# One core, two transformer-like blocks: second down-projection token-major, smaller opening pieces, heads of a pair in turn, a clamp moved to GpSimd

## The chip, the cores and the metric

The kernel runs on one core of one Trainium2 chip. The metric is the device time of one execution in microseconds; the median of three runs of the kernel before is 856.59 us (856.45 to 857.29). Engines are named as the profile names them: PE (TensorE), PEld (its weight loads), DVE (VectorE), ACT (ScalarE), POOL (GpSimd), SP (SyncE, which issues most transfers).

## The reference, cut to what matters

256 tokens of width 1024, all in float32, pass two blocks one after the other. The parts that the change touches:

```python
# first block: the input projection of the gated recurrence
h = rms_norm(x, norm_mix_pre)
z = h @ w_in                     # split into q, f_fwd, f_bwd, i, g, u, v, ga, gb
f = lb + (1 - lb) * sigmoid(zf)  # a gate per direction
logf = log(maximum(f, tiny))     # the clamp
k = (1 - lb) * sigmoid(-zf)
# second block: two attentions of 8 heads each (head width 64; queries and keys 64 or 96 wide)
out_a = dilated_attention(qa, ka, va, rel_bias)
out_b = causal_block_attention(qb, kb, vb)
h = h + concat(out_a, out_b) @ w_o
# second block: the last feed-forward part
hn = rms_norm_2(h, norm_ffn_g)
hid = square(relu(hn @ w_ff1))   # 256 x 4096
return h + hid @ w_ff2           # 256 x 1024
```

## The kernel before, in words

Weights come as 133 units of 128 x 2048 float32 (1 MB each), in the order in which they are used. SP issues their transfers into `raw`, a ring of four slots; unit u waits until unit u-4 is used. Each unit is split into two float32r parts: ACT copies it to `whi` (`split_hi`, L451), DVE subtracts to get `wlo` (`split_lo`, L906). The activations are split in the same way into `xh` and `xl`. PE then makes three products for each block: hi by hi, hi by lo, lo by hi. `ahead(u)` splits the unit three places ahead.

Most products are channel-major: a 128 x 128 block of the weights is loaded and 256 tokens stream past (`mm3`, L1641 to L1643). Some are token-major: 128 tokens of the activations are loaded and 512 weight columns stream past (`token_major`, L1707 to L1713, and `token_down`, L1903 to L1905). In the wide form (`wide_tiles`, L2009 and L2010) hi and lo activations stream together, 512 columns, followed by 256 for `wlo`.

**Opening.** SP issues half of x (512 KB), two halves of unit 0, the other half of x, two halves of unit 1, then whole units. ACT makes `xh` (L476) and `whi` (L502), DVE `xl` (L955) and `wlo` (L987), PE starts with 26 idle products on a tile of ones (L1763) and then runs `first_products`, 48 token-major products for units 0 and 1 (L1752 to L1758). Units 2 and 3 (`zu`) follow channel-major, block by block with all three products together, so they need `wlo` of the unit at their first block. The norm's statistics and its broadcast (`norm_stats`, `norm_bc`) stand inside unit 2 and behind it. Behind unit 4 comes `spatial_mix` (L1779), which needs `vn` from a DVE chain that begins with BN_STATS (L1019).

**Recurrence.** Eight heads in two groups. The kernel walks a tree of 8 levels: behind the PE work of unit 10 + lv stands level lv of group 0, behind unit 19 + lv that of group 1. For a level PE makes 64 small products (L1787; the trace holds a part of their records), DVE copies the masked result (L1068) and multiplies queries and decays (L1043, L1049), ACT gathers keys (`both_ways`, L540) and POOL updates the keys (`keys_update`, L381). While the levels of group 0 run, units 12 to 15 bring group 1's gates: DVE scales the product (`scaled`, L965), ACT makes sigmoids and the affine part (L482, L579, L585, L587), DVE clamps (`gates`, L1034). In DVE's order the clamp of unit u stands behind `ahead(u)` and ahead of `scaled` of unit u+1. ACT's order in an iteration u is `both_ways` for level u-10, `ahead(u)`, then the gate of unit u.

**Heads.** Pairs p = 0 to 7 of heads. `qk(p)` (L2169, L2170) makes logits, DVE adds the bias and takes the maximum (`logits_row`), ACT exponentiates (L783), DVE normalises (L1372, L1373), PE turns the probabilities (`turn`, L2179), ACT copies them, PE multiplies by the values (`pv`, L2197 to L2199). The products of a pair use two halves of the array: rows 0 to 63 and 64 to 127 in `qk` of the first four pairs, columns 0 to 63 and 64 to 127 in `pv`. In program order all products of the first head stand ahead of those of the second.

**Last feed-forward part.** 16 pairs of hidden tiles. Step j makes pair j by one wide unit and adds pair j-1 to the output by `down`, channel-major, 48 products of 256 columns into banks 3 to 6. Since relu and square pass a factor through, the norm's factor is applied at the end: its statistics are taken at step 13, its factor is turned to a row and broadcast (`norm_bc`, L1737), squared (L1622) and multiplied in. The last unit (`last_down`) finishes bank by bank; for each bank DVE scales (L1629) and adds the residual (L1630), and SP sends 256 KB (L345).

## Time and profile before

| | before |
|---|---|
| median of three runs | 856.59 us |
| the profiled execution's own time | 856.04 us |
| its span, first to last instruction | 854.3 us |
| PE busy | 845.0 us (99%) |
| DVE busy | 602.7 us (71%) |
| ACT busy | 461.3 us (54%) |
| POOL busy | 93.2 us (11%) |
| granted TensorE clock | 1.000 of full |

Matmuls are pipelined, so the busy time of PE includes overlap: what one product costs in a row of products is the distance between two starts, not the duration in a row. Such distances are taken from the timeline or from stages bounded by two starts. A matmul of float32 operands leaves two records here (52 for 26 idle products), one of float32r operands leaves one.

### The profile page before, as it was taken

To read this page: it belongs to the slowest core of one execution; us is meant where nothing else is said; L and a number is where in the kernel's file an instruction comes from. 1 tells how busy PE (TensorE), PEld (TensorE's weight loads), DVE (VectorE), ACT (ScalarE), POOL (GpSimd) and SP (SyncE) were. 2 spreads that over 40 slices of the span, in tenths; PEclk is the share of its full clock that TensorE was granted. 3 is DMA by queue.
4 is the path that set the end of the run, shared out by engine and by line. 5 is a ranking of instruction groups with operands and counts; after the bars stand their busy time and mean duration, and the time that the engine had idled before them with its cause. 6 is when DMAs were issued, how large, how long until landed. Compare 5 with 4: busy or idle time off the path is not lost.

```text
span 854.3 us, 14691 instructions
## 1 busy us (share of the span) xinstructions
PE 845.0 (99%) x6376; PEld 785.9 (92%) x6376; DVE 602.7 (71%) x761; ACT 461.3 (54%) x573; POOL 93.2 (11%) x71
## 2 busy tenths in 40 slices
PE   9999999999999999999999999999999999999998
PEld 8999988999999898888888799998998999999997
DVE  6967995884866586666666787778778775566554
ACT  7578764654344475445444574476566654444441
POOL 1002450661000000000000000000441000000000
PEclk9999999999999999999999999999999999999999
DMA  8745433442454555555555554544221555555451
GB/s 326 256 150 181 142 130 141 149 149 99 161 183 163 201 165 188 190 197 195 177 181 191 194 199 164 189 148 148 100 99 51 195 188 169 188 199 189 169 184 50
DMA packets 21264, 143.88 MB, mean 168 GB/s; under 512 B 2594, under 2 KB 2610, under 8 KB 4688
## 3 DMA queue, kind: packets, MB, share of 16 engines
q1 hardware_dynamic: 20016, 139.47, 47.1%
q0 software_dynamic: 1040, 3.43, 1.2%
q8 instruction: 50, 0.82, 0.4%
q14 instruction: 14, 0.11, 0.1%
q10 hardware_dynamic: 144, 0.04, 0.0%
HBM read 141.87 MB, written 1.06 MB: 167 GB/s over the span
## 4 chain that ended last, share of the span: by engine, by line
PE 83%; DVE 2%; ACT 1%; issue 0%; POOL 0%; DVEq 0%; ACTq 0%
PE ps L2009 14%; PE ps L1641 13%; PE ps L1643 12%; PE ps L1642 12%; PE ps L2010 7%; PE ps L1903 2%; PE ps L1905 2%; PE ps L1904 2%; PE ps L1787 1%; PE ps L1707 1%; PE ps L1713 1%; PE ps L1710 1%; PE ps L1667 1%; PE ps L1668 1%; PE ps L1672 1%; PE ps L1918 1%
## 5 line engine op out<-in xcount | busy, mean ns | idle before, releaser
L906 DVE TENSOR_TENSOR wlo<-raw,whi 128x2048 fp32r<-128x2048 f32 x129 | 297.3, 2307 | 73.8 <-ACT whi L451 72.4
L1641 PE MATMUL ps<-xx,whi 128*128 128x256 f32 x1144 | 330.5, 289 | 0.4 <-DVE wlo L906 0.4
L1642 PE MATMUL ps<-xx,whi 128*128 128x256 f32 x1144 | 324.1, 283 | 0.0
L1643 PE MATMUL ps<-xx,wlo 128*128 128x256 f32 x1144 | 324.0, 283 | 0.0
L451 ACT ACTIVATE whi<-raw 128x2048 fp32r<-128x2048 f32 x129 | 246.2, 1911 | 120.2 <-DMA raw<-w 120.2
L1641 PEld LDWEIGHTS ps<-xx,whi 128*128 128x128 f32 x1144 | 219.1, 192 | 3.5 <-issue 1.5
L1642 PEld LDWEIGHTS ps<-xx,whi 128*128 128x128 f32 x1144 | 219.3, 192 | 0.2
L1643 PEld LDWEIGHTS ps<-xx,wlo 128*128 128x128 f32 x1144 | 219.1, 192 | 0.0
L2009 PE MATMUL ps<-xx,whi 128*128 128x512 f32 x512 | 180.8, 397 | 0.0
L2010 PE MATMUL ps<-xx,wlo 128*128 128x256 f32 x512 | 143.8, 281 | 0.0
L2009 PEld LDWEIGHTS ps<-xx,whi 128*128 128x128 f32 x512 | 96.2, 188 | 22.5 <-issue 0.4
L2010 PEld LDWEIGHTS ps<-xx,wlo 128*128 128x128 f32 x512 | 97.0, 189 | 0.3
L1236 DVE TENSOR_TENSOR work<-ps,work 128x256 f32<-128x256 f32 x64 | 26.9, 421 | 65.1 <-ACT work L668 64.7
L381 POOL TENSOR_TENSOR work<-work 128x512 f32<-128x512 f32 x28 | 56.7, 2044 | 112.6 <-DVE work L1060 52.8
L668 ACT ACTIVATE work<-ps 128x256 f32<-128x256 f32 x64 | 23.9, 374 | 48.6 <-PE ps L2010 48.6
L672 ACT ACTIVATE xx<-work 128x512 fp32r<-128x512 f32 x27 | 17.1, 633 | 57.6 <-DVE work L1258 26.9
L965 DVE TENSOR_TENSOR work<-ps,bcs 128x512 f32<-128x512 f32 x34 | 23.4, 688 | 21.6 <-PE ps L1643 19.7
L1903 PE MATMUL ps<-whi,xx 128*128 128x512 f32 x88 | 34.5, 392 | 0.0
L1905 PE MATMUL ps<-wlo,xx 128*128 128x512 f32 x88 | 34.4, 391 | 0.0
L1904 PE MATMUL ps<-whi,xx 128*128 128x512 f32 x88 | 34.4, 391 | 0.0
L482 ACT ACTIVATE work<-work 128x512 f32<-128x512 f32 x26 | 16.4, 631 | 27.2 <-DVE work L965 27.0
L363 POOL TENSOR_TENSOR rtok<-eps_s,half_s 128x2 f32<-128x2 f32 (+1 forms) x5 | 3.9, 771 | 238.3 <-DVE eps_s L932 238.3
(275 smaller groups left out, 1002.5 us busy)
## 6 DMA issues: line engine op xcount, KB each, us to landing
raw<-w SPq DMA_DIRECT2D x129, 1024.0 KB, 4.9
raw<-w SPq DMA_DIRECT2D x4, 512.0 KB, 8.1
x<-xT SPq DMA_DIRECT2D x2, 512.0 KB, 6.1
work<-bias_scratch POOLq DMA_DIRECT2D x1, 1024.0 KB, 8.1
out<-x SPq DMA_DIRECT2D x4, 256.0 KB, 2.3
work<-lnr POOLq DMA_DIRECT2D x1, 512.0 KB, 3.6
work<-sgw POOLq DMA_DIRECT2D x1, 512.0 KB, 4.4
lvl_s<-lvl POOLq DMA_DIRECT2D x1, 448.0 KB, 4.8
```

Source lines behind the costliest of these rows:

```text
L381: ins = nc.gpsimd.tensor_tensor(v, v, pair[:, :, 1 - d:2 - d].broadcast_to([P, n, half]), ALU.mult)
L451: A(whi[:, slot, :], raw[:, slot, :], ACT.Copy).then_inc(sem("hi_ready"), 1)
L906: V.tensor_tensor(wlo[:, slot, :], raw[:, slot, :], whi[:, slot, :].bitcast(F32), ALU.subtract)\
L1236: return V.tensor_tensor(out[:, m, :], ps[banks[m]][:, 0:T], low[:, m, :], ALU.add)
L1641: mm(out, hi, xh[:, tile, :], start=start, stop=False, skip_group_check=skip)
L1642: mm(out, hi, xl[:, tile, :], start=False, stop=False, skip_group_check=skip)
L1643: return mm(out, wlo[:, slot, at:at + width], xh[:, tile, :], start=False, stop=stop, skip_group_check=skip)
L1903: mm(o, xh[:, base + kk, xs], whi[:, slot, wc], start=first, stop=False, skip_group_check=True)
L1904: mm(o, xl[:, base + kk, xs], whi[:, slot, wc], start=False, stop=False, skip_group_check=True)
L1905: return mm(o, xh[:, base + kk, xs], wlo[:, slot, wc], start=False, stop=end, skip_group_check=True)
L2009: mm(o[:, :], whi[:, u % SLOTS, w], xx[:, base + k, :, :], start=k == 0, stop=False)
L2010: last = mm(o[:, 0:T], wlo[:, u % SLOTS, w], xh[:, base + k, :], start=False, stop=k == 7)
```

## The change

1. **Opening.** SP sends x in four quarters, unit 0 in four quarters and unit 1 in two halves, in turn (`first_piece`). ACT, DVE and PE follow the same pieces; each product run needs one x quarter and one piece. The idle products go from 26 to 17. DVE folds the squares before it splits unit 2, and splits unit 4 behind the four `lb` operations; ACT evacuates `zv` before it splits unit 4. Units 2 and 3 run all products with `whi` first and those with `wlo` last (`first_parts`), with the statistics and the broadcast inside them.
2. **Clamp.** The four clamps of group 1's gates go from DVE to POOL, one behind each of the key updates of levels 3 to 6 of group 0 (`keep_in_range`); DVE's `prep` of group 1 waits for all four. Group 0's four stay on DVE.
3. **Heads.** `qk` and `pv` issue their products for the two heads in turn.
4. **Last part.** `down` is replaced by `token_down`, 24 products of 512 columns. The norm's factor stays a per-token scalar: DVE squares it (`r2`), `norm_bc` and L1622 go. The end has five parts: ACT scales and copies a part out of its bank, PE turns it (4 or 2 blocks of 128 x 128), DVE adds the residual, SP sends it (rows of 512 bytes; 256 KB three times, 128 KB twice).
5. Some semaphores are shared (`tile_fac`, `tile_eps`, `tile_turned`), which changes no order.

The diff, cut to its core:

```diff
 
...
+
+def first_piece(i):
+
+
+    if i < 4:
+        return 0, slice(512 * i, 512 * i + 512)
...
-            sp.dma_start(x[:, 0:4, :], xT[:, 0:4, :]).then_inc(sem("x_in"), 16)
-            for u in range(2):
-                for half in range(2):
-                    cols = slice(half * UNIT // 2, (half + 1) * UNIT // 2)
-                    sp.dma_start(raw[:, u, cols], w[stored(u)][:, cols]).then_inc(sem(f"raw_half{2 * u + half}"), 16)
-                if u == 0:
-                    sp.dma_start(x[:, 4:8, :], xT[:, 4:8, :]).then_inc(sem("x_in2"), 16)
+            for k, pieces in enumerate(((0, 1), (2, 3), (4,), (5,))):
+                sp.dma_start(x[:, 2 * k:2 * k + 2, :], xT[:, 2 * k:2 * k + 2, :]).then_inc(sem(f"x_in{k}"), 16)
+                for i in pieces:
+                    u, cols = first_piece(i)
+                    sp.dma_start(raw[:, u, cols], w[stored(u)][:, cols]).then_inc(sem(arrival(i)), 16)
...
-            for b in range(4):
-                sp.wait_ge(sem("out_ready"), b + 1)
-                sp.dma_start(out[:, 2 * b:2 * b + 2, :], x[:, 2 * b:2 * b + 2, :]).then_inc(sem("out_sent"), 16)
-            sp.wait_ge(sem("out_sent"), 64)
+            for i, (s, m, n, _) in enumerate(OUT_PARTS):
+                sp.wait_ge(sem("out_ready"), i + 1)
+                ts = slice(s * P, (s + 1) * P)
+                sp.dma_start(out[:, m:m + n, ts], x[:, m:m + n, ts]).then_inc(sem("out_sent"), 16)
...
+
+            def keep_in_range(part, m):
+
+
+                pool.wait_ge(sem("gates"), k_index(U_Q[1] + 2 + 2 * part + m) + 1)
+                fm = G[1]["F"][part][:, 2 * m:2 * m + 2, :]
+                nc.gpsimd.tensor_scalar(fm, fm, TINY, 1.0, ALU.max, ALU.min).then_inc(sem("in_range"), 1)
 
             for g in range(2):
                 for lv in range(1, 8):
                     keys_update(g, lv)
+                    if g == 0 and 3 <= lv <= 6:
+                        keep_in_range((lv - 3) // 2, (lv - 3) % 2)
...
+            for k, pieces in enumerate(((0, 1), (2, 3), (4,), (5,))):
+                act.wait_ge(sem(f"x_in{k}"), 16)
                 gained_hi("n1", "mix_pre", 0, k)
+                for i in pieces:
+                    first_hi(i)
...
-            split_hi(4)
 
             act.wait_ge(sem("rtok"), 1)
             for s in range(2):
                 evac(U_ZV + s, zv[:, s, :], ACT.Gelu, scale=rtok[:, 0, s:s + 1])
+            split_hi(4)
...
-            bc_copy("n6")
+            act.wait_ge(sem("r2"), 1)
+            for i, (s, m, n, _) in enumerate(OUT_PARTS):
+                b = 2 * s + m // 4
+                if b < 3:
+                    act.wait_ge(sem("out_bank"), b + 1)
+                elif m == 4:
+                    filled(UNITS - 1)
+                at = m % 4 * P
+                A(otok[:, s, m * P:(m + n) * P], ps[TOKEN["out"][b]][:, at:at + n * P], ACT.Copy, scale=r2[:, s:s + 1])\
+                    .then_inc(sem("out_scaled"), 1)
...
-            split_lo(2)
             link(V.tensor_tensor(sq1[:, 0:2, :], sq1[:, 0:2, :], sq1[:, 2:4, :], ALU.add))
             V.tensor_tensor(sq1[:, 0, :], sq1[:, 0, :], sq1[:, 1, :], ALU.add).then_inc(sem("folded"), 1)
+            split_lo(2)
+            norm_factors("n1", 0)
             split_lo(3)
-            norm_factors("n1", 0)
-            split_lo(4)
             dve.wait_ge(sem("gam_exp"), 1)
...
+            split_lo(4)
...
+                    if g:
+                        dve.wait_ge(sem("in_range"), 4)
                     for d in range(2):
                         V.tensor_tensor(H["Q"][d], H["q"], H["F"][d], ALU.mult).then_inc(sem(f"q_init{g}"), 1)
...
-                if u == U_ZI - 1:
-                    gates(1, 1, 1)
...
-                    if part and r < 5:
+                    if g == 0 and part and r < 5:
                         gates(g, part - 1, m)
...
-                    norm_factors("n6", 4)
-
-            dve.wait_ge(sem("norm_bcs"), before("bcs", "n6") + 1)
-            link(V.tensor_tensor(bcs[:, :], bcs[:, :], bcs[:, :], ALU.mult))
+                    dve.wait_ge(sem("norm_stats"), before("st", "n6") + 1)
+                    V.tensor_scalar(eps_s[:, 0:2], ps[7][:, 0:2], EPS, None, ALU.add).then_inc(sem("eps_added"), 1)
+                    dve.wait_ge(sem("rtok"), 5)
+                    V.tensor_tensor(r2, rtok[:, 4, 0:2], rtok[:, 4, 0:2], ALU.mult).then_inc(sem("r2"), 1)
+
...
+            for i, (s, m, n, bank) in enumerate(OUT_PARTS):
+                dve.wait_ge(sem("out_turned"), i + 1)
+                xs = x[:, m:m + n, s * P:(s + 1) * P]
+                V.tensor_tensor(xs, xs, ps[bank][:, 0:n * P].rearrange("p (n t) -> p n t", t=P), ALU.add).then_inc(sem("out_ready"), 1)
...
+                u, cols = first_piece(i)
+                ks = range(i, i + 1) if i < 4 else range(2 * i - 4, 2 * i - 2)
+                wc = {k: slice(cols.start + 512 * n, cols.start + 512 * n + 512) for n, k in enumerate(ks)}
+                pairs = [(s, k) for s in range(2) for k in ks]
...
+                pe.wait_ge(sem("act_hi"), ks[0] // 2 + 1)
+                pe.wait_ge(sem("hi_ready" if whole else "first_hi"), count)
                 for s, k in pairs:
-                    mm(o[s], xh[:, 2 * quarter + k, xs[s]], whi[:, u, wc[k]], start=quarter == 0 and k == 0, stop=False)
-                pe.wait_ge(sem("act_lo"), quarter + 1)
+                    mm(o[s], xh[:, k, xs[s]], whi[:, u, wc[k]], start=k == 0, stop=False)
+                pe.wait_ge(sem("act_lo"), ks[0] // 2 + 1)
                 for s, k in pairs:
-                    mm(o[s], xl[:, 2 * quarter + k, xs[s]], whi[:, u, wc[k]], start=False, stop=False)
-                pe.wait_ge(sem(("first_lo", "lo_ready")[half]), u + 1)
+                    mm(o[s], xl[:, k, xs[s]], whi[:, u, wc[k]], start=False, stop=False)
+                pe.wait_ge(sem("lo_ready" if whole else "first_lo"), count)
                 for s, k in pairs:
-                    last = mm(o[s], xh[:, 2 * quarter + k, xs[s]], wlo[:, u, wc[k]], start=False, stop=quarter == 3 and k == 1)
+                    last = mm(o[s], xh[:, k, xs[s]], wlo[:, u, wc[k]], start=False, stop=k == 7)
                 return last
...
+            def first_parts(u, base, inside):
+
+
+                bank_free(u, u % RING)
+                pe.wait_ge(sem("hi_ready"), u + 1)
+                w = lambda m, k: slice((8 * m + k) * P, (8 * m + k + 1) * P)
+                o = [ps[u % RING][:, m * T:(m + 1) * T] for m in range(2)]
+                blocks = [(m, k) for m in range(2) for k in range(8)]
+                for m, k in blocks:
+                    mm(o[m], whi[:, u % SLOTS, w(m, k)], xh[:, base + k, :], start=m == 0 and k == 0, stop=False, skip_group_check=True)
+                    mm(o[m], whi[:, u % SLOTS, w(m, k)], xl[:, base + k, :], start=False, stop=False, skip_group_check=True)
+                    if m and k == 0:
+                        inside()
+                arrived(u)
+                for m, k in blocks:
+                    last = mm(o[m], wlo[:, u % SLOTS, w(m, k)], xh[:, base + k, :], start=False, stop=k == 7, skip_group_check=True)
+                used(last)
+
             pe.wait_ge(sem("warm_set"), 1)
-            for n in range(26):
+            for n in range(17):
                 mm(ps[3 + n // 4 % 4][:, (n % 4) * P:(n % 4 + 1) * P], wtile, wtile, start=True, stop=True)
-            first_products(0)
-            used(first_products(1))
-            first_products(2)
-            used(first_products(3))
+            for i in range(6):
+                last = first_products(i)
+                if i in (3, 5):
+                    used(last)
...
-                    if u == U_ZU:
-                        steps.append(lambda: norm_stats("n1", sq1))
+                    if u in (U_ZU, U_ZU + 1):
+                        first_parts(u, 0, (lambda: norm_stats("n1", sq1)) if u == U_ZU else lambda: norm_bc("n1"))
+                        continue
                     if u == U_GB + 2:
                         steps.append(heads_bc)
                     two_tiles(u, 0, between=lambda: [step() for step in steps],
                               beside=(lambda i: heads_stats(i)) if u == U_GB else (lambda i: heads_stats(16 + i)) if u == U_GB + 1 else None)
-                if u == U_ZU:
-                    norm_bc("n1")
...
-                for hh in range(2):
-                    h = 2 * (p % 4) + hh
-                    o = ps[HEADS_BANK[p]][64 * hh:64 * hh + 64, 0:T]
-                    PT = probsT[:, 2 * (p % 2) + hh, :]
-                    hv = slice(64 * h, 64 * h + 64)
-                    mm(o[:, 0:P], v[:, 0, hv], PT[:, 0:P], start=True, stop=True)
-                    mm(o[:, P:T], v[:, 0, hv], PT[:, P:T], start=True, stop=False)
-                    last = mm(o[:, P:T], v[:, 1, hv], PT[:, T:384], start=False, stop=True)
+
+                for part in range(3):
+                    for hh in range(2):
+                        h = 2 * (p % 4) + hh
+                        o = ps[HEADS_BANK[p]][64 * hh:64 * hh + 64, 0:T]
+                        PT = probsT[:, 2 * (p % 2) + hh, :]
+                        hv = slice(64 * h, 64 * h + 64)
+                        if part == 0:
+                            mm(o[:, 0:P], v[:, 0, hv], PT[:, 0:P], start=True, stop=True)
+                        elif part == 1:
+                            mm(o[:, P:T], v[:, 0, hv], PT[:, P:T], start=True, stop=False)
+                        else:
+                            last = mm(o[:, P:T], v[:, 1, hv], PT[:, T:384], start=False, stop=True)
...
-                used(down((u + 1) % SLOTS, 8 + 2 * ((j - 1) % 3), j == 1))
+                for kk in range(2):
+                    for b in range(4):
+                        last = token_down("out", (u + 1) % SLOTS, 8 + 2 * ((j - 1) % 3), b, kk, j == 1 and kk == 0, False)
+                used(last)
+
+            def out_turned(i):
+
+                s, m, n, bank = OUT_PARTS[i]
+                pe.wait_ge(sem("out_scaled"), i + 1)
+                for k in range(n):
+                    last = nc.tensor.transpose(ps[bank][:, k * P:(k + 1) * P], otok[:, s, (m + k) * P:(m + k + 1) * P], ident)
+                last.then_inc(sem("out_turned"), 1)
...
-                if j == PAIRS2 - 2:
-                    norm_bc("n6")
             arrived(UNITS - 1)
             pe.wait_ge(sem("hid2_lo"), PAIRS2)
-            last_down((UNITS - 1) % SLOTS, 8 + 2 * ((PAIRS2 - 1) % 3), "out_bank")
+            for b in range(4):
+                for kk in range(2):
+                    last = token_down("out", (UNITS - 1) % SLOTS, 8 + 2 * ((PAIRS2 - 1) % 3), b, kk, False, kk == 1)
+                if b < 3:
+                    last.then_inc(sem("out_bank"), 1)
+                else:
+                    used(last)
+                if b == 2:
+                    out_turned(0)
+                    out_turned(1)
+            for i in range(2, len(OUT_PARTS)):
+                out_turned(i)
```

**What moves, on DVE and POOL, behind units 12 and 13.** `work<-ps,bcs` is the scaling of the next unit's product, L1034 the clamp. DVE before:

```order
L1049 TENSOR_TENSOR work<-work 128x256 x2
L906 TENSOR_TENSOR wlo<-raw,whi 128x2048
L1034 TENSOR_SCALAR work<-work 128x512
L965 TENSOR_TENSOR work<-ps,bcs 128x512
L1068 COPY_PREDICATED work<-lvl_s,ps 128x4x128 x2
```

and now:

```order
L1079 TENSOR_TENSOR work<-work 128x256 x2
L936 TENSOR_TENSOR wlo<-raw,whi 128x2048
L995 TENSOR_TENSOR work<-ps,bcs 128x512
L1100 COPY_PREDICATED work<-lvl_s,ps 128x4x128 x2
L1073 TENSOR_TENSOR work<-work 128x128x4 x2
```

The clamp no longer stands between the split and the scaling. On POOL now (L399 the key updates of levels 3 to 5, L407 the clamp):

```order
L399 TENSOR_TENSOR work<-work 128x128x4 x2
L407 TENSOR_SCALAR work<-work 128x512
L399 TENSOR_TENSOR work<-work 128x64x8 x2
L407 TENSOR_SCALAR work<-work 128x512
L399 TENSOR_TENSOR work<-work 128x32x16 x2
```

Behind each level's two updates stands one clamp.

**On PE, the first `pv`.** Before:

```order
L2197 MATMUL ps<-work 64x128
L2198 MATMUL ps<-work 64x128
L2199 MATMUL ps<-work 64x128
L2197 MATMUL ps<-work 64x128
L2198 MATMUL ps<-work 64x128
L2199 MATMUL ps<-work 64x128
```

and now:

```order
L2232 MATMUL ps<-work 64x128 x2
L2234 MATMUL ps<-work 64x128 x2
L2236 MATMUL ps<-work 64x128 x2
```

The same six products; the two heads alternate.

**On PE, the end of the program.** L1950 to L1952 are `token_down`, L2399 the transposes:

```order
L1950 MATMUL ps<-whi,xx 128x512
L1951 MATMUL ps<-whi,xx 128x512
L1952 MATMUL ps<-wlo,xx 128x512
L2399 MATMUL ps<-cst_s,work 128x128 [waits out_scaled]
L2399 MATMUL ps<-cst_s,work 128x128 x3
L2399 MATMUL ps<-cst_s,work 128x128 [waits out_scaled]
L2399 MATMUL ps<-cst_s,work 128x128
L2399 MATMUL ps<-cst_s,work 128x128 [waits out_scaled]
L2399 MATMUL ps<-cst_s,work 128x128
L216 UNCONDITIONAL_BRANCH
```

Before, the last rows were L1641 to L1643, channel-major, and nothing of PE's stood behind them.

## Rows read from the trace of the kernel before

**Rows 1.** Who waited for whom on PE, whole span: us in total, times, longest us.

```profile
PE ps L1787 <- ACT work L540: 1.5, 3, 0.9
PE ps L2179 <- DVE work L1373: 0.7, 2, 0.4
```

**Rows 2.** The timeline of the opening: start us, us, engine, line, op, out<-in [idle before].

```profile
1.06 7.40 PE L1763 MATMUL ps<-work 128*128 128x128 f32 x52 [1.06 <-DVE work L979]
...
5.03 1.71 ACT L476 ACTIVATE xx<-x,par_s 128x256 fp32r<-128x256 f32 x4 [2.36 <-DMA par_s<-par]
...
7.47 1.06 ACT L502 ACTIVATE whi<-raw 128x1024 fp32r<-128x1024 f32 x1 [0.73 <-DMA raw<-w]
...
8.67 1.16 PE L1752 MATMUL ps<-whi,xx 128*128 128x512 f32 x4 [0.21 <-ACT whi L502]
...
10.34 1.71 ACT L476 ACTIVATE xx<-x,par_s 128x256 fp32r<-128x256 f32 x4 [0.23 <-DMA x<-xT]
...
13.85 1.99 ACT L512 ACTIVATE work<-x 128x1024 f32<-128x1024 f32 x2
...
17.85 1.92 ACT L451 ACTIVATE whi<-raw 128x2048 fp32r<-128x2048 f32 x1 [0.20 <-DMA raw<-w]
...
20.19 0.36 PE L1641 MATMUL ps<-xx,whi 128*128 128x256 f32 x1 [0.39 <-DVE wlo L906]
```

**Rows 3.** The timeline of DVE and PE, units 3 to 5.

```profile
27.87 1.42 DVE L1019 BATCH_NORM_STATS2 nt<-work 128x6 f32<-128x512 f32 x2
...
36.56 2.28 DVE L906 TENSOR_TENSOR wlo<-raw,whi 128x2048 fp32r<-128x2048 f32 x1
...
38.50 1.97 PE L1779 MATMUL ps<-work 128*64 128x128 f32 x32
```

**Rows 4.** The source line of the clamps: duration ns min/median/max, first and last start us.

```profile
L1034 DVE TENSOR_SCALAR work<-work x8: 427/857/1378, 57.8 to 120.1; 128x512 f32<-128x512 f32 x8
```

**Rows 5.** The timeline of DVE and PE, units 13 and 14.

```profile
98.44 1.38 DVE L1034 TENSOR_SCALAR work<-work 128x512 f32<-128x512 f32 x1
...
99.85 0.69 DVE L965 TENSOR_TENSOR work<-ps,bcs 128x512 f32<-128x512 f32 x1
...
104.86 1.15 PE L1787 MATMUL ps<-work 128*64 128x64 f32 x32 [0.94 <-ACT work L540]
```

**Rows 6.** The timeline of POOL: key updates of level 4, group 0, then group 1.

```profile
104.95 3.15 POOL L381 TENSOR_TENSOR work<-work 128x512 f32<-128x512 f32 x2 [4.11 <-ACT work L540]
...
169.52 4.28 POOL L381 TENSOR_TENSOR work<-work 128x512 f32<-128x512 f32 x2 [2.35 <-DVE work L1049]
```

**Rows 7.** The timeline of PE, the first `pv`, and its next product.

```profile
597.55 0.43 PE L2197 MATMUL ps<-work 128*64 128x128 f32 x2
...
597.83 0.32 PE L2197 MATMUL ps<-work 128*64 128x128 f32 x1
...
598.63 0.39 PE L1641 MATMUL ps<-xx,whi 128*128 128x256 f32 x1
```

**Rows 8.** The windows of one `token_down` of block one and one `down` of block two.

```profile
core 0: us, PE busy (x) PEld busy (x) DVE busy (x) ACT busy (x) POOL busy (x), PEclk, DMA share, GB/s
457.45:462.93 5.48, 5.48 (x27) 4.50 (x25) 3.79 (x5) 2.27 (x4) 0.00 (x0) 1.00 0.55 191
678.41:684.18 5.77, 5.77 (x51) 5.77 (x50) 5.56 (x7) 2.42 (x4) 0.00 (x0) 1.00 0.55 179
```

**Rows 9.** The timeline of PE at `norm_bc` of the last norm.

```profile
832.45 0.61 PE L1737 MATMUL ps<-cst_s,rx 128*128 128x128 f32 x4
```

**Rows 10.** The timeline of the end.

```profile
847.38 4.55 SPq L345 DMA_DIRECT2D out<-x  x4
...
849.84 0.28 PE L1643 MATMUL ps<-xx,wlo 128*128 128x256 f32 x1
```

**Rows 11.** The page, part 5: operations of 256 columns on DVE and ACT.

```profile
L1236 DVE TENSOR_TENSOR work<-ps,work 128x256 f32<-128x256 f32 x64 | 26.9, 421 | 65.1 <-ACT work L668 64.7
...
L668 ACT ACTIVATE work<-ps 128x256 f32<-128x256 f32 x64 | 23.9, 374 | 48.6 <-PE ps L2010 48.6
```

125 lines of the change are left out of this document (49 added, 76 removed).

## The prediction

> **What bounds the kernel now.** I read the engines' busy time first: PE is busy for 99% of the span, so a gain must shorten PE's own row of products, its start, its end, or one of its few waits. Next I read PE's waits [rows 1]. They are small: 1.5 us at the level products of the recurrence, behind ACT's gathering of keys, and 0.7 us at the turning of probabilities, behind DVE. Then the timeline of the opening and of the end, where PE is not fed or no longer works [rows 2, 10], then the timelines around each changed place. The reader should look at starts: 48 products of 512 columns take 0.227 us each from start to start in the opening, a product of 256 columns 0.120.
>
> Durations come from one execution of 856.04 us, 0.55 below the median of 856.59. The sum is made on 856.04, and 0.55 is added at the end.
>
> **1. Opening.** PE runs idle products until 8.5 and its first real one at 8.67. It waits for ACT's copy of the first half unit, which landed at 7.47; ACT itself began at 5.03, when the parameters had come [rows 2]. Half of x (0.5 MB) was there by then, 1 MB by 7.47, 2 MB by 10.34 and 5 MB by 17.85 (the rows in which ACT waited for a DMA). Now PE's first product needs a quarter of x and a quarter unit, 0.5 MB, which is there by 5.0. ACT scales two tiles (0.43 us each, 1.71 for four) and copies 512 columns (half of 1.06). Starting at 4.5 to 5.0, that gives 5.9 to 6.4. The 17 idle products end at 1.06 + 17 x 7.40/26 = 5.9. From there 48 x 0.227 = 10.9 us of products would end at 16.8. But the last piece is 3 MB deep, landing at about 12.8 between the rows for 2 and 5 MB, and on the way PE waits two or three times for a piece, some 0.8 us in all: 17.6. Unit 2 needs ACT's copy: 12.8, plus 1.06 for the last piece, 1.99 for the squares, 1.9 for the copy, is 17.8. So unit 2 starts at about 17.9, not at 20.19: 2.3 us earlier. Its `wlo` is now needed only after 32 products (3.8 us), which covers DVE's folding and its split. With the old order inside the unit, that split would be waited for.
>
> What is late next is DVE. It has the same work between the squares and BN_STATS, and can begin it only when the squares are done, at 15.9, much as before. I put BN_STATS at 27.3, against 27.87 [rows 3]. All behind it moves by the same 0.55, so `wlo` of unit 5, ready at 36.56 + 2.28 = 38.84 before, is ready at 38.3. PE, 2.3 us earlier, wants it at 38.50 + 1.9 - 2.3 = 38.1. It waits about 0.25. **-2.05 us.** Bounds: -0.4, if smaller transfers land so late that only the 0.39 us wait at 20.19 goes; -2.7, if DVE gains as much as PE.
>
> **2. Clamp.** The timeline shows the clamp of unit 12's gates on DVE at 98.44 for 1.38 us and the scaling of unit 13's product directly behind it, at 99.85 [rows 5]. By the timeline PE had ended unit 13 at 96.6, so DVE was 3.2 us late. ACT needs that scaled product, makes its gate and only then gathers the keys of level 4: PE starts level 4 at 104.86, 0.94 idle. Start to start the wait is 1.0; at levels 5 and 6 the same measure gives 0.3 and 0.4. Without 1.3 us on DVE each of these is covered: scaling at 98.5, gathering done at 103.4, needed at 103.9. **-1.7 us.** What POOL adds is four one-input operations of 512 columns that no row shows. Two-input ones on 512 columns take 3.15/2 to 4.28/2 us [rows 6]. Below 2.1 the clamp is free: POOL idles 2.3 to 4.1 us between levels, and the clamp runs beside ACT's gathering. I take 1 us. The key updates may lengthen to group 1's 4.28, where DVE has no clamp and PE does not wait. Bounds: -2.0 (all of [rows 1]'s wait and a bit) and +0.3.
>
> A row worth seeing here: the same clamp takes 0.43 us at its shortest and 1.38 at its longest [rows 4]. The short four lie ahead of the first key update, the long four, from 98.44 on, beside them. The page "GPSIMD Engine Reference" of the Trainium skill, section "Engine selection", says that elementwise max on a tile belongs on VectorE, not on GpSimd. By that rule the term would be a loss, up to case (d) below. The rows stand against it: DVE pays 1.3 us, not 0.43, for keeping the clamp, and POOL has room.
>
> **3. Heads.** In `pv` the second head's first record starts 0.27 us behind the first head's (597.55 and 597.83), then both run together and the next product starts at 598.63, 1.08 after the first [rows 7]. In turn, both should start together: 0.8. In `qk` of the first four pairs the two heads' records already start 13 ns apart, and in the others all rows of the array are used: nothing. Not every 0.27 counts. From 604 to 655.6 DVE and ACT's exponentials work without a gap, and PE waits for them at the last two turns (0.7 us [rows 1]). So `pv` 1 to 5 make PE wait longer there, except that DVE waits at 651.87 for a `qk(7)` that can now start 0.3 earlier. `pv` 0, 6 and 7 count in full: 0.8 + 0.3. **-1.1 us.** Bounds: 0 and -2.2 (8 x 0.27).
>
> **4. Last part.** A `token_down` unit takes 5.48 us from start to start, a `down` unit 5.77 [rows 8]; over all units of each kind it is 5.50 and 5.757. 15 x 0.255 = **-3.8 us**. Bounds: -4.7, at 24 x 0.227 as in the opening, and -3.4. DVE and ACT have 4 us of room in each step, so nothing of theirs surfaces. `norm_bc` goes: 0.36 from 832.45 to the next start plus 0.09 at its edge, **-0.45 us** [rows 9]. `r2` takes two small operations on DVE, hidden.
>
> **5. The end.** Before: last product ends 850.1, two DVE operations, last issue at 851.6, span end at 854.3 [rows 10]. Counted from the first product of the last unit (844.2), that is 10.05. Now 18 products of 0.229 (4.1), 8 transposes of 0.11 with 0.26 at the edges (1.15), 6 products: the last ends at 6.8. Then ACT copies twice 256 columns (0.37, the second 0.3 behind), PE turns two blocks (0.11 each and 0.27 to the end), DVE adds 512 columns, 256 and 256 (0.69, 0.42, 0.42 [rows 11]; in a row): the last issue is at 8.75, not 7.4. From issue to end it was 2.65, for 256 KB. The last transfer has 128 KB but queues behind two others in rows of 512 bytes. 8.75 + 2.8 = 11.55: **+1.5 us**. Bounds: +0.9 and +2.6. No row shows a packet of 512 bytes. The page "DMA: Bandwidth & Descriptors" of the Trainium skill, section "Specifications", puts the smallest transfer at line rate at 512 bytes; by that the queue costs nothing and the term would be +1.1.
>
> Sum: -2.05 - 1.7 - 1.1 - 3.8 - 0.45 + 1.5 = -7.6; 856.04 - 7.6 = 848.4, and with 0.55, **849.0 us**.
>
> **Rivals.** (a) The smaller transfers come no faster than the halves did: the first parameters already kept ACT until 5.03, and below 5 us the transfers were at their slowest. PE then starts at 7.5 or waits as long in between. Gain 0.4 in place of 2.05: 850.6. (b) More goes right: `pv` counts eight times because DVE's chain moves too, and `token_down` runs at 0.227: -1.1 and -0.9, 847.0. For it, the last wide unit in front of some units is shorter; against it, 13 units of block one at 5.50. (c) The end is dear: five parts pass three engines and short rows leave slowly; +2.6 in place of 1.5, 850.1. (d) The other side: POOL's clamp is long. It stands between the key updates of levels 3 to 6, on which ACT's gathering and the next level wait. A level has 7.0 us, an update 4.3, so above 2.7 us each clamp delays the next level. To eat 7.6 us four clamps must take 4.6 us each. Against: no operation of POOL on 512 columns took more than half of that on average [rows 6]. If it holds, 857 or more. The rule of the Trainium skill's "GPSIMD Engine Reference" named under 2 speaks for this case. (e) The two heads do not run together in turn, because the array takes them in program order anyway: the records of `qk` show that it does not; if so, 850.1.
>
> **Chances.** Forecast 0.58, (a) 0.14, (b) 0.12, (c) 0.10, (d) 0.02, (e) 0.04. The range reaches down to (b) with the opening at its bound of -2.7 (847.0 - 0.65 = 846.3) and up to (a) and (c) together (849.0 + 1.65 + 1.1 = 851.8). About 0.2% (1.7 us) is what a measurement of this kernel can tell from no change. Below 854.9 lie all cases but (d): faster 0.96, same 0.02, slower 0.02.
>
> **What would show it.** Right: first `first_products` record at about 6, first product of unit 2 near 17.9, a wait of a few tenths at unit 5; no idle time at levels 4 to 6 and no DVE clamp above 0.5 us; `pv` at 0.8 from first product to the next; `token_down` units at 5.5 behind 672; the span ending 4.7 us behind the last 512-column product, not 4.2. Wrong: a start of unit 2 beyond 19, idle time at levels 4 to 7 with POOL clamps over 2.7 us, a granted clock below 1.0 in the first 20 us now that PE starts with less idle work and short waits, or PE waiting for DVE or transfers in the last part.

## The result, and the profile after

The changed kernel took 851.25 us in the median of four runs (851.04 to 854.09), the kernel before 856.53; the ratio is 0.9946 (0.9931 to 0.9960). Three more measurements beside the kernel before gave 850.87 against 856.54, 850.78 against 856.63, 850.66 against 856.85. So it gains 5.3 to 6.2 us where 7.6 were forecast. The median 851.25 lies inside the forecast range, near its upper end; the ratio times 856.53 gives 851.9, just above it. The one execution of 854.09 us does that: it lifts the mean of the four from 851.2 to 851.9.

The first profile of the change is of its longest execution, 854.09 us. It is 3 us longer than the other three and shows where the change is fragile. The page and PE's waits of that execution:

```profile
span 852.3 us, 13921 instructions
...
PE 841.1 (99%) x5986; PEld 764.4 (90%) x5986; DVE 594.9 (70%) x755; ACT 464.1 (54%) x579; POOL 102.4 (12%) x75
```

```profile
PE ps L1782 <- ACT whi L525: 1.8, 1, 1.8
PE ps L1835 <- ACT work L561: 1.2, 1, 1.2
PE ps L1811 <- DVE work L1009: 1.0, 1, 1.0
PE ps L2211 <- DVE work L1403: 0.7, 2, 0.4
PE ps L1835 <- DVE work L1073: 0.5, 1, 0.5
```

PE's busy time fell by 4 us, POOL's rose by 9, DVE's fell by 8. The three waits behind the gathering of keys [rows 1], at levels 4 to 6, are gone. New are a wait of 1.8 us in the opening and two in the recurrence, of 0.5 us at level 2 and 1.2 at level 3 (L1835 is the line of the level products). The timeline of that opening (start us, us, engine, line, operation [idle before]):

```profile
6.65 0.70 PE L1782 MATMUL ps<-whi,xx 128*128 128x512 f32 x2
...
11.54 0.91 ACT L501 ACTIVATE xx<-x,par_s 128x256 fp32r<-128x256 f32 x2 [1.80 <-DMA x<-xT]
...
14.16 1.28 PE L1782 MATMUL ps<-whi,xx 128*128 128x512 f32 x4 [1.80 <-ACT whi L525]
...
15.24 1.91 PE L1785 MATMUL ps<-whi,xx 128*128 128x512 f32 x4
...
21.32 0.28 PE L1800 MATMUL ps<-xx,whi 128*128 128x256 f32 x1
```

and the windows behind the wait (us; busy and instructions of PE, PEld, DVE, ACT, POOL; granted clock; DMA share; GB/s):

```profile
15.00:18.50 3.50, 3.50 (x10) 2.73 (x9) 2.92 (x6) 3.50 (x4) 0.00 (x0) 0.51 1.01 426
19.00:21.30 2.30, 2.30 (x11) 1.88 (x10) 2.23 (x4) 2.12 (x2) 0.93 (x2) 1.00 0.34 135
```

PE starts 2.0 us earlier than before [rows 2]. Then it stands idle for the third quarter of x. From 15.06 to 18.47, behind that idle time, the granted clock is at the lower of its two levels (1.2 GHz; 0.51 in the window), and a product of 512 columns takes 0.427 us from start to start, not 0.227. Unit 2 starts at 21.32, 1.1 us later than before. The rest of what this execution is slower by comes at levels 2 and 3; the last paragraph of the next section is on that.

A second profile of the same kernel is of an execution at the median (850.86 us); comparisons below use it unless they name another. Its opening:

```profile
5.77 1.17 PE L1811 MATMUL ps<-work 128*128 128x128 f32 x9
...
6.69 0.71 PE L1782 MATMUL ps<-whi,xx 128*128 128x512 f32 x2
...
10.94 0.91 ACT L501 ACTIVATE xx<-x,par_s 128x256 fp32r<-128x256 f32 x2 [1.32 <-DMA x<-xT]
...
12.41 1.06 ACT L525 ACTIVATE whi<-raw 128x1024 fp32r<-128x1024 f32 x1 [0.56 <-DMA raw<-w]
...
13.61 1.16 PE L1782 MATMUL ps<-whi,xx 128*128 128x512 f32 x4 [1.17 <-ACT whi L525]
...
19.24 0.36 PE L1800 MATMUL ps<-xx,whi 128*128 128x256 f32 x1
```

The wait is still there, 1.2 us, with the clock at 1.00 behind it. In the recurrence no wait above 0.13 us is left. Unit 2 starts at 19.24, against 20.19 before and 17.9 in the forecast.

### The profile page after: what moved, and what is told of

The parts are those of the page before. It is cut to its first block, busy times and chain, and to the rows that moved or that the text cites. A ratio compares the mean times of both kernels' runs of the same rounds, so it can differ in the third digit from the quotient of the medians.

```text
span 852.3 us, 13921 instructions
## 1 busy us (share of the span) xinstructions
PE 841.1 (99%) x5986; PEld 764.4 (90%) x5986; DVE 594.9 (70%) x755; ACT 464.1 (54%) x579; POOL 102.4 (12%) x75
## 3 DMA queue, kind: packets, MB, share of 16 engines
HBM read 141.87 MB, written 1.06 MB: 168 GB/s over the span
## 4 chain that ended last, share of the span: by engine, by line
PE 82%; DVE 4%; ACT 2%; issue 1%; POOL 0%; ACTq 0%
PE ps L2035 14%; PE ps L1668 9%; PE ps L1669 9%; PE ps L1670 9%; PE ps L2036 7%; PE ps L1950 6%; PE ps L1951 6%; PE ps L1952 6%; PE ps L1835 2%; PE ps L1734 1%; PE ps L1737 1%; PE ps L1740 1%; PE ps L1694 1%; PE ps L1699 1%; PE ps L1695 1%; ACT work L804 1%
## 5 line engine op out<-in xcount | busy, mean ns | idle before, releaser
L1668 PE MATMUL ps<-xx,whi 128*128 128x256 f32 x856 | 248.3, 290 | 0.4 <-DVE xx L1407 0.4
L1669 PE MATMUL ps<-xx,whi 128*128 128x256 f32 x856 | 242.1, 283 | 0.0
L1670 PE MATMUL ps<-xx,wlo 128*128 128x256 f32 x856 | 242.0, 283 | 0.0
L1668 PEld LDWEIGHTS ps<-xx,whi 128*128 128x128 f32 x856 | 164.0, 192 | 2.7 <-DVE xx L1407 0.7
L1669 PEld LDWEIGHTS ps<-xx,whi 128*128 128x128 f32 x856 | 164.2, 192 | 0.2
L1670 PEld LDWEIGHTS ps<-xx,wlo 128*128 128x128 f32 x856 | 163.9, 192 | 0.0
L2036 PE MATMUL ps<-xx,wlo 128*128 128x256 f32 x512 | 143.7, 281 | 0.0
L2035 PEld LDWEIGHTS ps<-xx,whi 128*128 128x128 f32 x512 | 96.2, 188 | 23.7 <-issue 0.3
L2036 PEld LDWEIGHTS ps<-xx,wlo 128*128 128x128 f32 x512 | 96.7, 189 | 0.8
L1950 PE MATMUL ps<-whi,xx 128*128 128x512 f32 x216 | 84.6, 392 | 0.0
L1951 PE MATMUL ps<-whi,xx 128*128 128x512 f32 x216 | 84.3, 390 | 0.0
L1952 PE MATMUL ps<-wlo,xx 128*128 128x512 f32 x216 | 84.2, 390 | 0.0
L399 POOL TENSOR_TENSOR work<-work 128x512 f32<-128x512 f32 x28 | 57.5, 2072 | 103.8 <-DVE work L1092 55.1
L1952 PEld LDWEIGHTS ps<-wlo,xx 128*128 128x128 f32 x216 | 40.5, 188 | 8.9
L1950 PEld LDWEIGHTS ps<-whi,xx 128*128 128x128 f32 x216 | 40.6, 188 | 8.8
L1951 PEld LDWEIGHTS ps<-whi,xx 128*128 128x128 f32 x216 | 40.6, 188 | 7.6
```

Source lines behind the costliest of these rows:

```text
L399: ins = nc.gpsimd.tensor_tensor(v, v, pair[:, :, 1 - d:2 - d].broadcast_to([P, n, half]), ALU.mult)
L1668: mm(out, hi, xh[:, tile, :], start=start, stop=False, skip_group_check=skip)
L1669: mm(out, hi, xl[:, tile, :], start=False, stop=False, skip_group_check=skip)
L1670: return mm(out, wlo[:, slot, at:at + width], xh[:, tile, :], start=False, stop=stop, skip_group_check=skip)
L1950: mm(o, xh[:, base + kk, xs], whi[:, slot, wc], start=first, stop=False, skip_group_check=True)
L1951: mm(o, xl[:, base + kk, xs], whi[:, slot, wc], start=False, stop=False, skip_group_check=True)
```

## The experiments

Unless said otherwise an edit is made on the changed kernel ("as changed"), and a median is of 5 runs (6 for the clamps back on DVE and for the old order).

**The changed kernel again**, three times on three chips, as the measure for its neighbours.

> The changed kernel unaltered, for a second profile. Theory A (the profiled execution of it was unlike its others: the third quarter of x landed at 11.5 us, PE waited 1.8 us and its clock was halved for 3.4 us behind that): median 851.2 us, and a profile, if it falls among the usual executions, without that wait: last of the first products near 17.5 to 18.3, clock 1.000, span 849.3. Theory B (PE waits like this in every execution, the smaller pieces come no sooner): the same wait of 1.5 us or more and first product of unit 2 at 20 us or later again, with the time at 854 or the rest of the kernel 3 us shorter than in the first profile.

> The changed kernel unaltered, once more, as the measure for the three kernels on the same chip: 850.9 us. Its first real product follows directly behind the last idle product, at the time that the clock's rise sets (6.6 us for a rise at 4.8 to 4.9 us, 7.4 us for one at 6.5 us).

> The changed kernel unaltered, as the measure for the three others on this chip: 850.8 us.

850.87, 850.78 and 850.66 us. Theory A's time is right, its profile without the wait is not: neither theory foresaw that the wait in the opening stays, only shorter (1.2, 0.9 and 0.5 us in the three profiles). Five runs below leave this opening as it is; their profiles show 0 to 1.5 us there. In the three profiles the first real product starts 0.03 us behind the start of the last idle one, at 6.69, 7.34 and 7.23.

**Group 1's clamps back on DVE.**

```diff
-                    if g == 0 and 3 <= lv <= 6:
-                        keep_in_range((lv - 3) // 2, (lv - 3) % 2)
...
-                    if g == 0 and part and r < 5:
+                    if part and r < 5:
```

> The changed kernel with group 1's four clamps back on DVE behind the split of each unit, everything else as changed. Theory A (the sum of the prediction, 1.7 us for the clamp): 1.7 us above the unaltered changed kernel, 852.9 us, with the waits at levels 3 to 6 as before. Theory B (on POOL the clamp takes 1.9 to 2.2 us, not 1, and the key updates and ACT's gathering behind it give part of it back): at most 0.8 us above, 852.0 us. Theory C (level 3 waits 1.1 us because of the opening's new order and not the clamp): the wait at level 3 stays in this run too.

852.93 us, 2.06 above. Theory A; in the traces the waits at levels 3 to 6 cost 1.9 us. The trace has the old pattern: the clamp of 1.39 us beside a key update, then level 4 late:

```profile
98.13 1.39 DVE L1055 TENSOR_SCALAR work<-work 128x512 f32<-128x512 f32 x1
...
104.56 1.15 PE L1826 MATMUL ps<-work 128*64 128x64 f32 x32 [0.95 <-ACT work L552]
```

And as changed, with the clamp on POOL and no idle time of PE at level 4:

```profile
96.05 3.73 POOL L399 TENSOR_TENSOR work<-work 128x512 f32<-128x512 f32 x2 [2.55 <-ACT work L561]
99.87 2.25 POOL L407 TENSOR_SCALAR work<-work 128x512 f32<-128x512 f32 x1
...
102.66 3.48 POOL L399 TENSOR_TENSOR work<-work 128x512 f32<-128x512 f32 x2 [0.55 <-ACT work L561]
...
102.99 1.15 PE L1835 MATMUL ps<-work 128*64 128x64 f32 x32
```

**The clamp twice**, to find where POOL becomes the bound.

```diff
-                nc.gpsimd.tensor_scalar(fm, fm, TINY, 1.0, ALU.max, ALU.min).then_inc(sem("in_range"), 1)
+                for n in range(2):
+                    if n:
+                        pool.wait_ge(sem("in_range"), 2 * (2 * part + m) + 1)
+                    nc.gpsimd.tensor_scalar(fm, fm, TINY, 1.0, ALU.max, ALU.min).then_inc(sem("in_range"), 1)
```

> The changed kernel with each of the four clamps on POOL done twice (the second pass changes no number), to find where POOL becomes the bound. POOL idles 0.55 to 1.0 us ahead of the key updates of levels 4 to 7 now and a clamp takes 1.9 to 2.2 us. Theory A (a clamp longer than the room delays the next key update, and with it ACT's gathering and PE's next level): about 1 us for each of three levels, 3 us above the unaltered changed kernel, 853.9 us, with PE waiting at levels 5 to 7. Theory B (the key update stands beside the level's products, so a late one is still in time): under 0.5 us above, 851.3 us.

852.76 us, 1.98 above the neighbour on the chip: theory A in kind, two levels instead of three. PE waits at levels 6 and 7, 0.9 and 1.1 us:

```profile
114.26 2.58 POOL L399 TENSOR_TENSOR work<-work 128x512 f32<-128x512 f32 x2
116.88 1.06 ACT L564 ACTIVATE work<-work 128x1024 f32<-128x1024 f32 x1 [0.55 <-POOL work L399]
116.93 5.19 POOL L410 TENSOR_SCALAR work<-work 128x512 f32<-128x512 f32 x2
117.99 1.15 PE L1838 MATMUL ps<-work 128*64 128x64 f32 x32 [0.88 <-ACT work L564]
```

Two clamps (5.2) and an update (2.6) fill 7.9 us from one update to the next, more than the 7.0 of a level. This is rival (d)'s mechanism, met at twice the work. A single clamp and its update take 5.2 to 6.1 us and stay hidden. The choice of engine that the Trainium skill advises ("GPSIMD Engine Reference", "Engine selection": elementwise max belongs on VectorE) would have cost 2 us here.

**The heads one behind the other**, twice (qk and pv as in the minus lines of the change).

```diff
-                for part in range(3):
-                    for hh in range(2):
...
+                for hh in range(2):
```

> The changed kernel with the products of qk and pv again one head behind the other. Theory A (1.1 us, of which pairs 0, 6 and 7 count in full): 852.3 us. Theory B (DVE's chain from 604 to 656 us sets the end of that stretch, so only pair 0 and pair 7 count): 0.5 us above the unaltered changed kernel, 851.7 us. In both, each pv 1.08 us long from its first product to the next stage's, and 0.8 us in the unaltered one.

853.53 us, 2.7 above, against both theories, but spread from 850.90 to 853.90. Its trace is only 0.8 us longer between 486 and 661. Ahead of that it is 1.9 us longer, 0.4 of it in the opening and 1.5 behind a late landing at 52 us (below). That is the profiled execution alone; why two others took as long no trace shows. So it was repeated:

> The changed kernel with qk and pv one head behind the other, beside the unaltered one on the same chip. Theory A (between 486 and 661 us the trace of the first such run is 0.8 us longer, the rest of its 2.7 us came from a unit that landed 1.5 us late at 52 us): 0.8 us above the unaltered changed kernel. Theory B (the order of the products of the heads moves the instruction fetches and so makes the late landing at 52 us the rule): 2 us above or more again, with the same wait of 1.2 us at level 3.

851.43 us, 0.65 above the neighbour, with overlapping spreads; between 577 and 658 us the trace is 0.87 longer. Theory A, by the trace more than by the medians. The wait at level 3 did not come back, so B is out. One `pv`, heads in turn:

```profile
595.82 0.44 PE L2232 MATMUL ps<-work 128*64 128x128 f32 x4
596.09 0.39 PE L2234 MATMUL ps<-work 128*64 128x128 f32 x4
596.31 0.39 PE L2236 MATMUL ps<-work 128*64 128x128 f32 x4
596.63 0.39 PE L1668 MATMUL ps<-xx,whi 128*128 128x256 f32 x1
```

and one head behind the other:

```profile
595.64 0.43 PE L2223 MATMUL ps<-work 128*64 128x128 f32 x2
595.91 0.27 PE L2224 MATMUL ps<-work 128*64 128x128 f32 x1
595.92 0.32 PE L2223 MATMUL ps<-work 128*64 128x128 f32 x1
...
596.72 0.39 PE L1668 MATMUL ps<-xx,whi 128*128 128x256 f32 x1
```

0.81 us from first product to the next stage's, and 1.08 [rows 7]. PE's 0.7 us of waits for the turning of probabilities is the same in both. The traces also show which pair gained nothing. As changed, `pv` 7 starts 1.04 us behind `pv` 6 and waits for ACT (third profile):

```profile
656.15 0.44 PE L2232 MATMUL ps<-work 128*64 128x128 f32 x4
...
657.19 0.44 PE L2232 MATMUL ps<-work 128*64 128x128 f32 x4 [0.15 <-ACT work L810]
```

With one head behind the other the same distance is 1.03 (656.63 to 657.66), without a wait.

**The last part as before.**

```diff
-                for kk in range(2):
-                    for b in range(4):
-                        last = token_down("out", (u + 1) % SLOTS, 8 + 2 * ((j - 1) % 3), b, kk, j == 1 and kk == 0, False)
-                used(last)
+                used(down((u + 1) % SLOTS, 8 + 2 * ((j - 1) % 3), j == 1))
```

with `last_down`, `norm_bc` and the end in four parts.

> The changed kernel with the last feed-forward part as before: down channel-major, norm_bc, the end in four parts of DVE scaling and adding. Theory A (token-major units 3.8 us shorter, norm_bc 0.45, the new end 1.5 us longer): 2.75 us above the unaltered changed kernel, 854.0 us. Theory B (the units give 3.3 us only, as the first profile of the change shows between 661 and 818 us, and the end costs 1.3): 2.4 us above, 853.6 us. Theory C (the end is dear, 2.6 us or more): 1.6 us above or less, 852.8 us.

853.15 us, 2.28 above, between theories B and C; the traces differ by 2.66 between 577 us and the end, which is between A and B. Windows as changed, one `token_down` and one wide unit:

```profile
675.86:681.37 5.51, 5.51 (x27) 4.51 (x25) 5.32 (x7) 2.40 (x4) 0.00 (x0) 1.00 0.56 193
681.37:687.01 5.64, 5.64 (x34) 4.90 (x32) 5.64 (x5) 3.39 (x4) 0.00 (x0) 1.00 0.52 186
```

and with `down`, the same and the next wide unit:

```profile
675.48:681.24 5.76, 5.76 (x50) 5.76 (x49) 5.56 (x7) 2.41 (x4) 0.00 (x0) 1.00 0.52 185
681.24:686.80 5.56, 5.56 (x35) 4.89 (x33) 5.56 (x5) 3.13 (x4) 0.00 (x0) 1.00 0.59 189
692.54:698.19 5.65, 5.65 (x34) 4.90 (x33) 2.85 (x3) 2.11 (x3) 0.00 (x0) 1.00 0.54 188
```

Behind the first of them each `token_down` unit takes 5.47, and the wide unit in front is now always 5.64, where it alternated between 5.65 and 5.56. Per step 0.29 - 0.04 = 0.25 us. The end, from the first product of the last wide unit (826.32 and 829.87) to the end of the span, is 22.78 and 21.53: 1.25 longer, of which one `token_down` hides 0.29, so 1.5 for the new end.

**The whole opening as before**, then only its pieces, then only its order.

> The changed kernel with the whole opening as before: halves of x and of units 0 and 1, 26 idle products, the old order of the splits, units 2 and 3 block by block. Theory A (the opening brings what the second profile of the changed kernel shows at spatial_mix, 37.55 us against 38.50): 0.95 us above the unaltered changed kernel's 850.9, so 851.8 us. Theory B (the 2.05 us of the prediction, hidden in the profile by some other wait): 852.9 us. Theory C (the other parts bring nearly all of the 5.7 us): 851.2 us or less.

851.74 us. Against the changed kernel on the same chip, measured later (850.66), it is 1.1 above, against the second profile's run 0.9. In the traces `spatial_mix` starts here and in the second profile at:

```profile
38.38 1.97 PE L1798 MATMUL ps<-work 128*64 128x128 f32 x32
37.55 1.97 PE L1827 MATMUL ps<-work 128*64 128x128 f32 x32
```

In the two other usual profiles of the changed kernel it starts at 37.91 and 37.43, so the opening brings 0.5 to 0.95 us. Theory A.

The next run takes back the pieces: halves and 26 idle products, with the new order kept.

> The changed kernel with the transfers and copies in halves again and 26 idle products, but with the new order of the splits and with units 2 and 3 in two passes. Theory A (smaller transfers start PE 2 us sooner, 6.7 against 8.7 us, but the bytes up to 3 MB come 1.4 us later than in halves, 14.3 against 12.9 us, so PE waits): the old pieces lose at most 0.6 us, 851.4 us, with first products from 8.7 to 19.7 us without a wait, and the last byte of unit 1 at 12.9 us. Theory B (the pieces bring nearly the whole gain of the opening): 851.8 us or more. Theory C (the pieces bring nothing, all of it is the order): 850.9 us.

850.91 us, which spoke for C, but the changed kernel had been measured on another chip. Beside each other:

> The changed kernel with the opening's old halves and 26 idle products but the new order, beside the unaltered one on the same chip. Theory A (the smaller pieces bring nothing, since PE waits for landings whichever way it starts): within 0.3 us of the unaltered changed kernel. Theory B (they bring 0.6 us or more, and the equal medians of the two earlier calls came from two chips): 0.6 us or more above it.

851.27 against 850.78 us, with spreads of 2.5 and 1.9 us in both. By the medians the pieces, with their fewer idle products, bring between 0 and 0.5 us; A and B cannot be told apart by this. The two profiles are of the longest and the second longest execution: the clock rose at 6.1 and 7.3 us, PE's first real product came at 9.3 and 9.8, and `spatial_mix` at 38.5 and 39.1, no sooner than with the whole old opening, where the clock rose at 4.0.

The last run of the three keeps the pieces and takes back the order.

```diff
             link(V.tensor_tensor(sq1[:, 0:4, :], sq1[:, 0:4, :], sq1[:, 4:8, :], ALU.add))
+            split_lo(2)
...
-            split_lo(2)
-            norm_factors("n1", 0)
             split_lo(3)
+            norm_factors("n1", 0)
+            split_lo(4)
```

> The changed kernel with the new pieces and 17 idle products, but with the splits of units 2 to 4 in the old order and units 2 and 3 block by block. Theory A (unit 2's split stands between the foldings and ends near 20.9 us, so PE, ready at 19.2, waits for it 1.6 us and the new pieces bring nothing): 852.4 us. Theory B (the order gives only the 0.4 us that PE waited at 20.19 before): 851.3 us.

(The hunk shows DVE's part: `split_lo(2)` goes back between the foldings, and units 2 and 3 are block by block again.) 853.96 us: 3.1 above, twice theory A. Unit 2 wants its `wlo` at its first block and waits for it:

```profile
19.94 2.29 DVE L936 TENSOR_TENSOR wlo<-raw,whi 128x2048 fp32r<-128x2048 f32 x1 [0.65 <-ACT whi L476]
...
22.38 0.36 PE L1668 MATMUL ps<-xx,whi 128*128 128x256 f32 x1 [2.89 <-DVE wlo L936]
```

So the new pieces with the old order are 2.2 us worse than the old opening (851.74): the split of unit 2 starts at 19.94, against 17.8 in the kernel before. The new order is what the pieces need: it brings 3.1 us with them, and by the medians 0.5 to 0.8 without them (851.27 and 850.91 against 851.74, spreads overlapping).

**26 idle products** in place of 17.

> The changed kernel with 26 idle products in place of 17, all else as changed. Theory A (the landings of x's third quarter and of unit 1 set the start of unit 2, PE's start does not): first real product at 8.5 us, no or nearly no wait at the third quarter, unit 2 at 19.4 to 19.8 us against 19.2 to 19.6, and at most 0.4 us above the unaltered changed kernel. Theory B (PE's start counts): 1.9 us later everywhere, 852.7 us.

851.66 us, 1.0 above: between the theories. In its profile the clock rose at 6.67 us, so the real products started at 9.54 and unit 2 at 20.53, 11.0 behind, without a wait:

```profile
9.54 0.70 PE L1782 MATMUL ps<-whi,xx 128*128 128x512 f32 x2
...
20.53 0.28 PE L1800 MATMUL ps<-xx,whi 128*128 128x256 f32 x1
```

In the other profiles with these pieces and the new order unit 2 came at 19.0 at the earliest. An estimate from that: a start of PE up to about 8.0 costs nothing, and a later one counts in full. With 26 idle products the small pieces (851.66) are no better than the halves (850.91 and 851.27), so by the medians what the pieces bring comes from the earlier start. Fewer than 17 idle products were not tried.

**The wait removed**: unit 1's first half in two transfers and copies, x's second half in one transfer.

```diff
-            for k, pieces in enumerate(((0, 1), (2, 3), (4,), (5,))):
-                sp.dma_start(x[:, 2 * k:2 * k + 2, :], xT[:, 2 * k:2 * k + 2, :]).then_inc(sem(f"x_in{k}"), 16)
+            for k, pieces in enumerate(((0, 1), (2, 3), (4, 5), (6,))):
+                if k < 3:
+                    ts = slice(2 * k, 2 * k + 2 if k < 2 else 8)
+                    sp.dma_start(x[:, ts, :], xT[:, ts, :]).then_inc(sem(f"x_in{k}"), 16)
```

> The changed kernel with the opening one step further: the first half of unit 1 in two transfers of 256 KB with copies of their own, and the second half of x in one transfer of 512 KB instead of two. Theory A (PE's wait of 1.2 us at 12 us is for the third quarter of x and for a copy of 1024 columns behind it; x comes at 10.5 us in place of 10.9 to 11.5 and the first copy takes 0.6 us instead of 1.06): unit 2 starts 0.8 us sooner, at 18.4, and 850.1 us. Theory B (the rows of 2 KB are what makes the transfers late, and one more such transfer makes all behind it later): no gain, 850.9 us or more, and unit 2 at 19.2 us or later.

> The opening with unit 1's first half in two transfers and x's second half in one, again, beside the unaltered changed kernel on one chip. Theory A (the third quarter of x and the copy of 1024 columns behind it were the wait): 0.6 to 0.8 us below the unaltered changed kernel. Theory B (the 0.7 us between the medians of the two earlier calls came from the chips): within 0.2 us.

850.14 us, and 849.83 beside 850.66 on one chip: 0.8 less. Theory A both times, though unit 2 starts at 18.8 and 18.7, not 18.4. The last byte of unit 1 lands at 13.5 and 13.1, against 14.2 to 14.9 as changed. No wait is left between 7.73 and unit 2:

```profile
7.73 0.70 PE L1784 MATMUL ps<-whi,xx 128*128 128x512 f32 x2
...
10.51 0.91 ACT L503 ACTIVATE xx<-x,par_s 128x256 fp32r<-128x256 f32 x2 [0.63 <-DMA x<-xT]
...
18.74 0.28 PE L1802 MATMUL ps<-xx,whi 128*128 128x256 f32 x1
```

This is the best kernel of the study, 0.992 of the kernel before (0.9907 to 0.9934). Part of what the opening gains is given back in the recurrence, at level 3, where PE now waits 0.4 us for ACT.

**The last issue by ACT**, on top of that.

> The same, and the last part of the output issued by ACT instead of SP. In the second profile of the changed kernel SP issues the last three parts at 845.12, 845.54 and 846.09, 0.4 to 0.5 us each in a row, while the last add ends at 845.76. Theory A (that row costs the end 0.3 us): 0.3 us below fine5x_b. Theory B (the transfer of the part before it ends last anyway, or a second queue starts dearer): no gain or 0.2 us above.

850.51 us, 0.7 above, with overlapping spreads. Theory B: ACT issues at 845.28, but the last landing is at 848.15 and the span ends 5.3 us behind the start of the last row of turnings (843.26), as with SP's row of issues. The row of issues was not what the end waited for.

**A late landing at 52 us.** In two profiles (the first of the change, and the first with the heads one behind the other) a unit landed 1.5 to 1.7 us late, and ACT's copy with it. In the second of them:

```profile
52.26 1.92 ACT L476 ACTIVATE whi<-raw 128x2048 fp32r<-128x2048 f32 x1 [5.00 <-DMA raw<-w]
...
97.87 1.15 PE L1835 MATMUL ps<-work 128*64 128x64 f32 x32 [1.19 <-ACT work L561]
```

and in the changed kernel's second profile:

```profile
50.37 1.92 ACT L476 ACTIVATE whi<-raw 128x2048 fp32r<-128x2048 f32 x1 [3.50 <-DMA raw<-w]
```

Fifteen of the transfer's sixteen parts had landed by 50.7, the sixteenth came at 52.2. The gates of group 0 and all of DVE's chain are later from there, and PE pays for it some 40 us later, with 0.4 us at level 2 and 1.2 at level 3 (0.5 and 1.2 in the first profile of the change). A transfer of instructions (one packet of 16 KB) ran in the same 2 us, but it did so too in the profile without the delay. What delays the one part stays open.

## Why the forecast was right or wrong

| term | forecast | medians | traces |
|---|---|---|---|
| opening | -2.05 | -0.9 to -1.1 | -0.5 to -1.1 |
| clamp | -1.7 | -2.06 | -1.9 |
| heads | -1.1 | -0.65 | -0.87 |
| last part, `norm_bc`, end | -2.75 | -2.28 | -2.66 |
| sum | -7.6 | -5.9 to -6.1 | -5.9 to -6.5 |

The sum of the parts is more than most measurements of the whole, 5.3 to 6.2 us. Matching products of the trace before and of the second profile give 0.95, 1.64, 0.83 and 2.6 us in the four places, 6.0 in all; but 0.9 of it is lost between 330 and 545 us, in stages that the change does not touch (0.45 and 0.3 in the third and fourth profile). A new wait of 0.2 us at 538 is part of it, in the second profile alone; the rest stays open.

**Opening: the step that failed.** The term of 2.05 us measured 0.5 to 1.1. PE was to start at 5.9 to 6.4, end its first products at 17.6 and start unit 2 at 17.9. That had three parts.
- "The 17 idle products end at 1.06 + 17 x 7.40/26 = 5.9" took a mean of two paces. Idle products start every 0.43 us at first and every 0.22 later; the change of pace comes where the trace's record of the granted clock at full begins. That rise was at 4.8, 4.9, 6.3 and 6.0 us in the four profiles of the changed kernel, and at 3.9 in the profile before. So the last of the 17 starts at 6.6 to 7.3, and the idle products, not the transfers, set the first product.
- "the last piece is 3 MB deep, landing at about 12.8" took the old transfers, whose last part landed at 12.86. In the first 15 us before and as changed:

```profile
DMA packets 1260, 4.83 MB, mean 322 GB/s; under 512 B 272, under 2 KB 288, under 8 KB 1072
```

```profile
DMA packets 1786, 4.46 MB, mean 298 GB/s; under 512 B 331, under 2 KB 347, under 8 KB 1643
```

 With more and shorter packets 5 to 8% less is moved by then, in four profiles. More weighs that a transfer counts only with the last of its sixteen parts, and one or two of them trail. Of the last piece the middle parts landed at 12.2 to 12.7, against 11.9 before, but the last part at 14.2 to 14.9, not 12.8. With x's second half in one transfer, and as many packets, it was 13.1 and 13.5. So the number of packets does not explain it; why parts trail stays open.
- "on the way PE waits two or three times for a piece, some 0.8 us in all" was one wait of 0.5 to 1.8 us, and behind the longest the clock fell. I named a clock below 1.0 as a sign of error, but gave it no price.

Unit 2 came at 19.1 to 19.6 in the three usual profiles. "I put BN_STATS at 27.3" failed with it: the squares were done at 17.2 to 17.7, not 15.9, and BN_STATS started at 28.3 to 28.8, later than before. That `spatial_mix` came sooner all the same shows that DVE's chain did not set it: the 0.25 us at unit 5 did not come up. Right was that with the old order inside the unit the split would be waited for (2.9 us in that run).

**Clamp: right, with a wrong size inside.** POOL takes 1.92 to 2.25 us for a clamp, not 1. By the forecast's own bound ("above 2.7 us each clamp delays the next level") that changes nothing, and the doubled clamp showed that bound at work. The key updates took 3.2 to 3.7 us, under the 4.28 allowed.

**Heads: right in kind.** 0.81 us as forecast; "`pv` 0, 6 and 7 count in full" gave 1.1, the traces 0.87, since `pv` 6 gained nothing: PE then waits for ACT at `pv` 7. Rival (e) is out.

**Last part: right.** 15 x 0.25 us, though as 0.29 gained on `token_down` and 0.04 lost on the wide unit in front, where the forecast had only 0.255 on the units themselves. `norm_bc` brought about 0.4 (0.45 forecast). The end cost 1.5 to 1.6 (1.5 forecast): 11.6 us from the first product of the last unit, against 11.55. The 1.1 us that the line rate of the Trainium skill's "DMA: Bandwidth & Descriptors" would have made of it is less than was measured, but no run sets the rows of 512 bytes apart.

**Rivals.** (a) was half true: its mechanism, transfers that do not come sooner, held (1 MB at 7.6 in the second profile and 7.45 before, then later than before from 1.75 MB on), but PE started sooner. (b), (c) and (d) did not come; (d) begins at twice the clamp.

## What to carry to other kernels

This opening was bound by the last byte that its first stage needs, as long as PE started before about 8 us: look at when the last part of each transfer lands before making the first pieces smaller, and give the last pieces the short copies. An earlier start that leads into idle time can cost more than it brought: in one of the ten profiles with these pieces and 17 idle products the clock fell behind it. When work moves to an idle engine, what counts is its room between two dependent steps, here 7 us per level, and doubling the moved work shows how near the bound is.
